# A row gather of an expert layer takes 4 experts of 32 tokens instead of 1 expert of 128 tokens

## What is computed

```python
q = (tb @ w_q).reshape(PEER_BLOCK, PEER_HEADS, 2, KEY_HALF)
s = jnp.einsum('thsk,hsnk->thsn', q, sub_keys)
sv, si = lax.top_k(s, PEER_TOPK)
cand = sv[:, :, 0, :, None] + sv[:, :, 1, None, :]
cidx = si[:, :, 0, :, None] * N_KEYS + si[:, :, 1, None, :]
top_s, pos = lax.top_k(cand.reshape(..., 256), PEER_TOPK)
idx = jnp.take_along_axis(cidx.reshape(..., 256), pos, axis=-1)
g = jax.nn.softmax(top_s, axis=-1)
act = jax.nn.gelu(jnp.einsum('thkd,td->thk', u_tab[idx], tb))
out = jnp.einsum('thk,thkd->td', g * act, v_tab[idx])
```

## Time and profile before

| what | value |
|---|---|
| median of 3 runs (4822.53 to 4825.95) | 4825.51 us |
| span of the profiled execution | 4824.5 us |
| TensorE busy, share of the span | 3951.6 us, 82% |
| VectorE busy | 2725.7 us, 56% |
| GpSimd busy | 1419.8 us, 29% |
| ScalarE busy | 679.6 us, 14% |
| moved by the gathers' queue | 1140.92 MB, 62.1% of 16 engines' span |

### The profile page before, as it was taken

How to read it: one execution, slowest core, us unless ns; L and a number is a source line. 1 busy time by engine, 2 the same in 40 slices (tenths; PEclk the granted TensorE clock), 3 DMA queues, 4 the chain that set the end, 5 groups by cost and what they waited for, 6 DMA issues and landing times.

```text
span 4824.5 us, 40811 instructions
## 1 busy us (share of the span) xinstructions
PE 3951.6 (82%) x9855; PEld 1849.3 (38%) x9855; DVE 2725.7 (56%) x6854; ACT 679.6 (14%) x1490; POOL 1419.8 (29%) x1570
## 2 busy tenths in 40 slices
PE   8999999999976677778777768768768768779998
PEld 5656666645642233233223223323223223222222
DVE  6463300014677666667667666666666666666553
ACT  2232300011011111011011011111111111101001
POOL 0464000000023333333333334333334433342221
PEclk8997999999988999889989999889999899897555
DMA  1110111012048999989989989989999998996663
GB/s 65 39 32 21 71 35 37 24 50 79 30 184 347 383 363 364 381 347 367 388 350 379 369 355 367 370 356 371 375 372 357 368 393 332 371 367 156 155 153 81
DMA packets 182776, 1206.41 MB, mean 250 GB/s; under 512 B 27024, under 2 KB 30608, under 8 KB 42640
## 3 DMA queue, kind: packets, MB, share of 16 engines
q0 software_dynamic: 157696, 1140.92, 62.1%
q1 hardware_dynamic: 24992, 64.53, 4.1%
HBM read 1199.31 MB, written 4.88 MB: 250 GB/s over the span
## 4 chain that ended last, share of the span: by engine, by line
PE 49%; DMA 21%; DVE 14%; issue 11%; POOL 3%; ACT 1%; DVEq 0%; SPq 0%; POOLq 0%; ACTq 0%
PE psC L706 22%; DMA ring<-in_uv,idxu 21%; PE psA L443 6%; PE psB L443 5%; PE psA L657 5%; POOL ring L416 3%; PE psB L727 3%; DVE ring L1373 2%; PE psC L645 1%; PE psB L645 1%; PE psC L471 1%; DVE dg L1365 1%; DVE hot L1348 1%; DVE hot L1346 1%; DVE pick L1350 1%
## 5 line engine op out<-in xcount | busy, mean ns | idle before, releaser
L706 PE MATMUL psC<-ring,dg 128*128 128x512 f32 (+1 forms) x4608 | 2449.0, 689 | 789.7 <-DVE dg L1365 789.6
L1373 DVE CUSTOM_DVE_ANT_0 ring<-ring,xn2c 128x1024 f32<-128x1024 f32 (+1 forms) x1152 | 1395.0, 1223 | 991.8 <-DMA ring<-in_uv,idxu 986.2
L416 POOL DMA_INDIRECT ring<-in_uv,idxu x1152 | 1231.3, 1069 | 2423.5 <-PE psC L706 2035.4
L706 PEld LDWEIGHTS psC<-ring,dg 128*128 128x128 f32 (+1 forms) x4608 | 937.0, 209 | 2277.6 <-issue 2276.5
L939 ACT ACTIVATE act<-dot 128x2 f32<-128x2 f32 (+1 forms) x576 | 117.3, 204 | 2852.3 <-DVE dot L1373 2851.2
L1365 DVE TENSOR_SCALAR dg<-ident,act,gw 128x128 f32<-128x128 f32 (+1 forms) x1152 | 339.8, 343 | 62.8 <-PE psC L706 62.8
L657 PE MATMUL psA<-xn2T,w_q 128*128 128x384 f32 (+1 forms) x768 | 238.3, 470 | 3.9 <-ACT xn2T L920 3.9
L407 POOL MEMSET sv<- 128x288 f32 x1 | 0.3, 338 | 624.8 <-DVE x L1265 624.8
L657 PEld LDWEIGHTS psA<-xn2T,w_q 128*128 128x128 f32 x768 | 144.6, 190 | 92.1 <-issue 5.8
L1252 DVE TENSOR_TENSOR sgb<-psB,sgb 128x384 f32<-128x384 f32 (+1 forms) x24 | 11.4, 529 | 222.7 <-PE psB L443 222.7
L727 PE MATMUL psB<-wgate,xn3T 128*128 128x512 f32 (+1 forms) x288 | 135.0, 595 | 0.0
(11 more groups left out here) (298 smaller groups left out, 2889.4 us busy)
## 6 DMA issues: line engine op xcount, KB each, us to landing
ring<-in_uv,idxu POOLq DMA_INDIRECT x1152
w_q<-in_w_q SPq DMA_DIRECT2D x16, 512.0 KB, 3.5
w_xb<-in_w_xb SPq DMA_DIRECT2D x8, 512.0 KB, 3.5
w_gb<-in_w_gb SPq DMA_DIRECT2D x8, 512.0 KB, 3.5
w_ga<-in_w_ga SPq DMA_DIRECT2D x8, 512.0 KB, 3.5
w_gp<-in_w_gp SPq DMA_DIRECT2D x8, 512.0 KB, 3.5
w_yb<-in_w_yb SPq DMA_DIRECT2D x8, 512.0 KB, 3.4
wout<-in_w_out SPq DMA_DIRECT2D x1, 4096.0 KB, 12.2
```

What stands on the lines that cost most here:

```text
L416: pool.indirect_dma_start(out=ring[0:rows, k % RING, :], out_offset=None, in_=a["uv"], in_offset=bass.IndirectOffsetOnAxis(ap=idxu[0:rows, ...
L706: ins = nc.tensor.matmul(acc[0:rows, 512 * half:512 * (half + 1)], dg[0:rows, k % 4, 0:rows], ring[0:rows, k % RING, D + 512 * half:D + 51 ...
L1373: ins = v.tensor_tensor_reduce(ring[0:rows, r, 0:D], ring[0:rows, r, 0:D], xn2c[0:rows, :], 1.0, 0.0, ALU.mult, ALU.add, dot[0:rows, k:k + 1])
```

## The change

A gather still has 128 rows of 8 KB and a slot still holds 128 partitions, but its partitions now are 4 experts (J) of 32 tokens (TOK). A tile is cut into slabs of 32 tokens, four in a full tile and two in the last. A round (t, h, q) covers experts 4q to 4q+3 of head h for all slabs: four gathers, or two in the last tile. There are 1024 gathers in the full tiles as before, and 64 in the last tile in place of 128 with 64 rows.

- The dot needs each slab's normed x four times, below each other: xrep, six slots, loaded by SyncE from DRAM (replicas). For this xn2 and x2 are stored to DRAM when they are made (store_x2), and x2 is read back per tile (x2c). The ring, now ten slots, takes their place in SBUF.
- In the diagonal's place stands a 128 x 32 matrix that is the identity of 32 four times below each other (eye) times coef, made for the four slabs by one instruction. Its product with v sums the four experts into the slab's 32 rows of acc: each slab has its own 32 columns of the array.
- TensorE's quad does a round's eight matmuls and frees all its slots at the last one. A round's diagonals are made behind the dots of the next round.
- The experts are chosen for two heads at a time (a batch), two batches ahead, one step behind each dot. choose(0) and choose(1) run ahead of the first gather, and all eight heads' best keys too. ScalarE brings numbers and gates into the new layout (spread).
- GpSimd, TensorE, ScalarE and VectorE have the expert layer written out without loops.

```diff
-RING = 8
+RING = 10
+J = 4
+TOK = P // J
+Q = TOPK // J
+SLABS = P // TOK
+REPS = 6
+LOOK = 2
...
+def slabs(t):
+
+    return rows_of(t) // TOK
+
+
+def first_gather(t, h=0, q=0):
+
+    return P * t + Q * slabs(t) * h + slabs(t) * q
+
+
+def round_of(t, h, q):
+
+    return HEADS * Q * t + Q * h + q
...
     ring = put("ring", [P, RING, 2 * D])
-    pT = put("pT", [P, 2, P])
-    put = region(RNG + 65536 + 1536, RNG + 65536 + 9728)
-    xn2c = put("xn2c", [P, D])
+    xrep = put("xrep", [P, REPS, D])
     cand = put("cand", [P, TOPK, TOPK])
     crep = put("crep", [P, TOPK, TOPK])
     hot = put("hot", [P, 2, TOPK, TOPK])
+    dg = put("dg", [P, 2, SLABS, TOK])
...
+        def store_x2(t):
+            n = rows_of(t)
+            sp.wait_ge(g.xn2_ok, t + 1)
+            sp.dma_start(a["x2_scr"][P * t:P * t + n, :], x2[0:n, t, :]).then_inc(g.x2_out, 16)
+            sp.dma_start(a["xn2_scr"][P * t:P * t + n, :], xn2s[0:n, t % 2, :]).then_inc(sem(f"xn2_out{t % 2}"), 16)
         for t in range(NT):
             if t >= 2:
                 sp.wait_ge(g.x2_ok, t - 1)
             sp.dma_start(xr[0:rows_of(t), t % 2, :], a["x"][P * t:P * t + rows_of(t), :]).then_inc(sem(f"xr_in{t % 2}"), 16)
+            if t >= 2:
+                store_x2(t - 2)
+        store_x2(NT - 2)
+        store_x2(NT - 1)
+        sp.wait_ge(g.x2_out, 16 * NT)
+        sp.wait_ge(sem("xn2_out0"), 16 * ((NT + 1) // 2))
+        sp.wait_ge(sem("xn2_out1"), 16 * (NT // 2))
...
+        def replicas(t, gr):
+            i = SLABS * t + gr
+            if i >= REPS:
+                u = i - REPS
+                sp.wait_ge(g.dot_ok, first_gather(u // SLABS, HEADS - 1, Q - 1) + u % SLABS + 1)
+            for j in range(J):
+                sp.dma_start(xrep[TOK * j:TOK * (j + 1), i % REPS, :],
+                             a["xn2_scr"][P * t + TOK * gr:P * t + TOK * (gr + 1), :]).then_inc(xrep_in[i % REPS], 16)
...
+        for gr in range(slabs(0)):
+            replicas(0, gr)
+        sp.dma_start(x2c[:], a["x2_scr"][0:P, :]).then_inc(g.x2c_in, 16)
+        for t in range(NT):
+            n = rows_of(t)
+            if t >= 1:
+                sp.wait_ge(g.ple_mm, t)
+            sp.dma_start(pT[:, :, 0:n], a["p_T"][:, :, P * t:P * t + n]).then_inc(g.pT_in, 16)
+            if t >= 1:
+                store(t - 1, P)
+            if t + 1 < NT:
+                m = rows_of(t + 1)
+                sp.wait_ge(g.x2c_used, t + 1)
+                sp.dma_start(x2c[0:m, :], a["x2_scr"][P * (t + 1):P * (t + 1) + m, :]).then_inc(g.x2c_in, 16)
+                for gr in range(slabs(t + 1)):
+                    replicas(t + 1, gr)
...
-        def gather(u, s, rows):
-
-            pool.wait_ge(g.idx_ok, u + 1)
-            for k in range(TOPK):
-                pool.wait_ge(g.slot_free, u * TOPK + (k + 1))
-                alone(pool)
-                pool.indirect_dma_start(
-                    out=ring[0:rows, k % RING, :], out_offset=None, in_=a["uv"],
-                    in_offset=bass.IndirectOffsetOnAxis(ap=idxu[0:rows, s, k:k + 1], axis=0),
-                ).then_inc(gathered[k % RING], 16)
-        with pool.Fori(0, (UNITS - HEADS) // 2) as w:
-            for s in range(2):
-                gather(w * 2 + s, s, P)
-        with pool.Fori((UNITS - HEADS) // 2, UNITS // 2) as w:
-            for s in range(2):
-                gather(w * 2 + s, s, TS)
+        pool.wait_ge(g.sc_mm, 2 * HEADS)
+        pool.wait_ge(g.x2_out, 16 * NT)
+        for t in range(NT):
+            for h in range(HEADS):
+                batch = 4 * t + h // 2
+                if h % 2 == 0:
+                    pool.wait_ge(g.idx_ok, batch + 1)
+                for q in range(Q):
+                    for gr in range(slabs(t)):
+                        n = first_gather(t, h, q) + gr
+                        if n >= RING:
+                            pool.wait_ge(g.slot_free, n - RING + 1)
+                        pool.indirect_dma_start(
+                            out=ring[:, n % RING, :], out_offset=None, in_=a["uv"],
+                            in_offset=bass.IndirectOffsetOnAxis(ap=idxq[:, batch % 3, h % 2, q, gr:gr + 1], axis=0),
+                        ).then_inc(gathered[n % RING], 16)
...
-        def experts(u, rows, last=False, between={}):
-
-            for k in range(TOPK):
-                pe.wait_ge(g.diag_ok, u * TOPK + (k + 1))
-                alone(pe)
-                for half in range(2):
-                    ins = nc.tensor.matmul(acc[0:rows, 512 * half:512 * (half + 1)], dg[0:rows, k % 4, 0:rows],
-                                           ring[0:rows, k % RING, D + 512 * half:D + 512 * (half + 1)],
-                                           start=False, stop=(last and k == TOPK - 1))
-                ins.then_inc(g.slot_free, 1)
-                for step in between.get(k, ()):
-                    step()
...
+        def quad(t, h, q):
+            n0 = first_gather(t, h, q)
+            pe.wait_ge(g.diag_ok, round_of(t, h, q) + 1)
+            b = q % 2
+            last = h == HEADS - 1 and q == Q - 1
             for half in range(2):
-                nc.tensor.matmul(acc[0:rows, 512 * half:512 * (half + 1)], ident[0:rows, 0:rows],
-                                 x2[0:rows, bass.ds(t, 1), 512 * half:512 * (half + 1)].rearrange("p a n -> p (a n)"),
-                                 start=True, stop=False)
-            first, second = {}, {}
-            if before:
-                turn, todo = embedding(t - 1, P)
-                first[6] = [turn]
-                for k in range(9, TOPK):
-                    first[k] = [todo.pop(0), todo.pop(0)]
-                for k in range(3):
-                    second[k] = [todo.pop(0), todo.pop(0)]
-                assert not todo
-            experts(t * HEADS, rows, between=first)
-            experts(t * HEADS + 1, rows, between=second)
-            with pe.Fori(1, HEADS // 2 - 1) as w:
-                for s in range(2):
-                    experts(t * HEADS + w * 2 + s, rows)
-            experts(t * HEADS + 6, rows)
-            experts(t * HEADS + 7, rows, last=True)
-            nc.tensor.transpose(psB[0:rows, 2, 0:rows], ident[0:rows, 0:rows], ident[0:rows, 0:rows]).then_inc(g.acc_done, 1)
+                for gr in range(slabs(t)):
+                    ins = nc.tensor.matmul(acc[TOK * gr:TOK * (gr + 1), 512 * half:512 * (half + 1)], dg[:, b, gr, :],
+                                           ring[:, (n0 + gr) % RING, D + 512 * half:D + 512 * (half + 1)],
+                                           start=False, stop=last, skip_group_check=True)
+            ins.then_inc(g.slot_free, slabs(t))
...
+                ins = nc.tensor.matmul(acc[0:rows, 512 * half:512 * (half + 1)], ident[0:rows, 0:rows],
+                                       x2c[0:rows, 512 * half:512 * (half + 1)], start=True, stop=False,
+                                       skip_group_check=True)
+            ins.then_inc(g.x2c_used, 1)
+            for h in range(HEADS):
+                for q in range(Q):
+                    quad(t, h, q)
+                    if t >= 1:
+                        if (h, q) == (0, 2):
+                            turn(t - 1, P)
+                        if (h, q) == (1, 0):
+                            ple(t - 1, P)
+                        if h == 1 and q < 4:
+                            gate3(t - 1, P, q)
...
+        def spread(n):
+            sc.wait_ge(g.sel_ok, n + 1)
+            if n >= 3:
+                sc.wait_ge(g.diag_ok, 2 * Q * (n - 2))
+            for gr in range(slabs(n // 4)):
+                for j in range(J):
+                    ins = nc.scalar.activation(
+                        selq[TOK * j:TOK * (j + 1), n % 3, :, :, :, gr],
+                        sel[TOK * gr:TOK * (gr + 1)].rearrange("p i s (q j) -> p i s q j", j=J)[:, :, :, :, j], ACT.Copy)
+            own(ins)
+            nc.scalar.activation(idxq[:, n % 3], selq[:, n % 3, 0], ACT.Copy).then_inc(g.idx_ok, 1)
...
-        with ve.Fori(0, HEADS - 1) as h:
+        with ve.Fori(0, HEADS) as h:
...
-        def diagonals(u, s, q, rows):
-            ve.wait_ge(g.act_ok, u * 8 + (q + 1))
-            for k in (2 * q, 2 * q + 1):
-                ve.wait_ge(g.slot_free, u * TOPK + (k + RING - 3))
-                v.tensor_scalar(dg[0:rows, k % 4, 0:rows], ident[0:rows, 0:rows], act[0:rows, k:k + 1],
-                                gw[0:rows, s, k:k + 1], ALU.mult, ALU.mult).then_inc(g.diag_ok, 1)
-
-        def unit(u, s, rows, between={}):
-            for q in range(TOPK // 2):
-                for k in (2 * q, 2 * q + 1):
-                    r = k % RING
-                    ve.wait_ge(gathered[r], u * 32 + 16 * (k // RING + 1))
-                    ins = v.tensor_tensor_reduce(ring[0:rows, r, 0:D], ring[0:rows, r, 0:D], xn2c[0:rows, :], 1.0, 0.0,
-                                                 ALU.mult, ALU.add, dot[0:rows, k:k + 1])
-                ins.then_inc(g.dot_ok, 1)
```

(106 more changed lines are left out.)

380 lines of the change are left out of this document (187 added, 193 removed).

## The result

The changed kernel takes **5558.15 us** (median of 4 runs, 5549.25 to 5568.73) against 4825.73 of the kernel before (4 runs beside it): a ratio of 1.153, 95% interval 1.151 to 1.155, so 15% slower. The forecast was 5866, in a range of 5200 to 6280. The profiled execution has a span of 5555.9 us.

A forecast was written before the change was run, and what follows sets the result against it. The prediction took gathers to bind the earlier kernel's full tiles, and one slot-release loop per round after the change: 1424 + 256 x 16.2 + 48 + 200 + 10 + 37 = 5866 us, range 5200 to 6280.

The forecast's parts named there:

- The loop: Full tiles: each round of four gathers holds one full slot-release loop, 16.2 us against 11.2 before.
- The signs it gave in advance: Changed profile: rounds about 16 us, gathers in bursts of four, DMA share about 0.6, clock 0.5 to 0.6, records spanning 3.5.
- from the diagonal to GpSimd's issue: Part of each round, from the diagonal's start to GpSimd's next gather issue: 5.05 us at half clock.
- Half clock: TensorE in each round's burst: 1.2 GHz, because it would be idle for some 12 us of each round.
- Selection step and coef: Between a round's last dot and its diagonal: 0.40 and 0.32 us, with the dot's 1.23 before them.
- Issue to the second dot: Part of each round, from GpSimd's issue to the dot of the second gather: 9.2 us, least 7.96, most seen 9.82.
- Fixed parts: Outside the rounds: first gather at 1424 us, last tile 200, its last round 10, the tail 37.
- The copies of x: Loads of x by DRAM in each tile: 0 us, since the queue idles a third of each round; up to 50 otherwise.
- the embedding: Previous tile's embedding, matmuls between rounds and VectorE's wait for gate3: 6 us per tile, 48 in all (0 to 100).
- Full clock: Rival for TensorE's bursts: 2.4 GHz, 3.26 instead of 5.05 us, round 14.4, total 5405 us; chance 0.12.
- Strict order: Rival for TensorE's column groups: 16 records in 9 steps instead of 4, round 20.5 us, total 6967; chance 0.08.
- Faster: Rival for the full tiles: the gather queue never runs dry, total 4270 to 4685 us; chance 0.05.

The follow-up runs named there:

- Runs 1 to 3: Three variants of the changed kernel: diagonals behind the next round's first dot, 4348.81 us; eight ring slots, 6804.45 us; eleven slots with four x copies, 4892.71 us.
- run 4: Changed kernel with ten idle matmuls into an unused bank behind each round's sums in the full tiles: 5445.6 us, ratio 1.128.
- run 6: Changed kernel with quad's two loops exchanged, so each column group's two matmuls follow each other: 5563.97 us, ratio 1.153.
- run 3: Changed kernel with eleven ring slots instead of ten and four x copies instead of six: 4892.71 us, ratio 1.013.
- run 1: Changed kernel with a round's diagonals behind the first dot of the next round instead of the fourth: 4348.81 us, ratio 0.900.
- run 5: Changed kernel with eight idle matmuls behind a round's sums, only in rounds away from the previous tile's embedding: 5533.68 us, ratio 1.146.

## Why the prediction was right

- **The loop was named and priced.** The forecast was a round that holds dot, diagonal, matmuls, issue and the landing of the second gather. Runs 1 to 3 show it from three sides: a shorter stay in the slots takes 1209 us off, one slot more 665, two slots less cost 1246. The signs it gave in advance are there: four gathers in a burst and then a wait for TensorE, where the earlier trace rows show single ones; clock 0.59 (0.5 to 0.6); 16 records in 3.6 us (3.5). Only the DMA share came out higher, 0.73 against about 0.6. The shorter round makes 0.66 of it (4 x 2.49 / 15.07); the rest is that an 8 KB packet lasts 338 ns on average in the full tiles, where it lasts 309 in the undisturbed stretch of the kernel before (3000 to 3004).
- **The term that was mis-sized: from the diagonal to GpSimd's issue**, 5.05 us from the earlier trace rows, measured 4.29. It makes 0.76 of the 1.1 us by which a round is shorter. Half clock was right (the records start 0.86 us apart), so the difference isn't the clock. The row held two diagonals of 0.60 us together and TensorE's first matmuls of a gather behind a selection; now one instruction of 0.29 makes the diagonals, and from there to the first matmul it is 0.35 instead of 0.49. From that matmul to the issue it is 3.94 instead of 4.56 (medians of 222 rounds and of 57 selections). The traces place most of this 0.62 on GpSimd: from TensorE's rise of slot_free to the issue it is 0.80 us before, with two small instructions between (one on a semaphore, one that adds for the loop's wait), and 0.26 us after, where the code without loops has none there. From the first matmul to that rise it is 3.77 and 3.68.
- **Selection step and coef**: 1.95 forecast, 1.74 measured. **Issue to the second dot**: 9.2 forecast, 9.11 measured. The estimate from the Trainium skill, DMA: Bandwidth & Descriptors, "Anatomy of one DMA", 4.4 us for one gather, is not what these runs show: from the issue to the first dot it is 5.72 us (median).
- **Fixed parts.** First gather 1431 (forecast 1424). From it to the last tile 3904 us (forecast 4195: 256 x 16.2 + 48). The last tile's sums end 183 us after it starts, where 200 + 10 was forecast; the tail is 37.8 (37). So 310 us too many in all: 291 in the full tiles, 27 in the last, less 7 at the start and 1 at the tail.
- **The copies of x weren't free.** The step said 0, at most 50 in all, because the queue is idle a third of the time. They cost 45: eight come in one burst and stand in front of a round's gathers, whose landing is on the loop. With 5.6 of a tile on them, 2 to 3 are left for the embedding (6 forecast); the total of a tile, 8 us over 32 rounds of 15.07, was near by two errors of opposite sign.
- **Rivals.** Full clock: the bursts ran at 0.50, and run 4 shows that the price put on it, 1.8 us of a round, is near the measured 1.5. Strict order: excluded, by the changed kernel and more strongly by run 6. What the Trainium skill, TensorE: Matmul & The Clock Gate, Part 3 "The mechanism", says, that matmuls start and end in program order, does not hold between column groups here (16 records in 3.5 us in either order). Faster: it needed a round under 12.1 us, and run 3 agrees with that point: a round of 12.3 gave 4893, just above the kernel before.

## What to carry to other kernels

When buffers are freed in groups, draw the loop from the last consumer of a group to the landing of the transfer it frees, and count how many transfers are still outstanding when it starts. If these and the freed one itself last shorter than the loop, every group pays about the difference. Here the loop is 1.74 + 4.29 + 5.72 = 11.75 us; with 0, 2 and 3 gathers outstanding (8, 10 and 11 slots) the estimate, 11.75 less 2.49 for each of these and for the freed one, is 9.3, 4.3 and 1.8 us over the 9.95 of a round without a gap; measured are 9.95, 5.1 and 2.3. The cure that was worth most here is to start the release earlier in program order, before adding buffers: one call moved by three dots turned a kernel 15% slower into one 10% faster, where one slot more brought it to 1% slower. Idle share of a queue is no cover for a transfer that is issued in a burst ahead of the one that the loop waits for.

## What was not expected of the hardware

- Matmuls on different column groups of TensorE start side by side even where a matmul that waits for its own group stands between them in the program: the starts of 16 records span 2.6 us in both orders (run 6).
- Copies of 32 rows of 4 KB into 32 partitions beside 8 KB row gathers lower what the same busy DMA engines move, from 421 to 285 GB/s; loads and stores of 128 partitions in the same 4 KB packets don't (426, both in run 1's kernel).
- After ten idle matmuls behind a round the next sums ran at 2.4 GHz in 154 of 222 rounds (run 4); with eight behind 22 of a tile's 32 rounds, in 11 of 222 (run 5); in the changed kernel, without them, in none.
- From a semaphore's rise to the gather that waits for it GpSimd takes 0.26 us when the gather itself waits (222 times in the changed kernel, all within 0.01) and 0.80 with two small instructions between (57 times in the kernel before).
